# Moving a group of conditioning products from the first layer's mixer into the second layer's attention

## The reference

```python
for l in range(DEPTH):
    mod = (silu_c @ ada_w[l] + ada_b[l])[:, None, :]
    sh1, sc1, g1, sh2, sc2, g2 = jnp.split(mod, 6, axis=-1)
    ...
    h_lat = modulate(x, sh1, sc1)
    h_ctx = modulate(ctx, csh1, csc1)
    ...                                   # l = 0: GLA and convolution, l = 1: attention
    x = x + g1 * o_lat
    ...
    y = hier_moe(modulate(x, sh2, sc2).reshape(-1, d_), *moe_params)
```

## Time and profile before

| | us |
|---|---|
| median of 3 runs | 1013.79 |
| lowest, highest run | 1010.34, 1020.07 |
| span of the profiled execution, first to last instruction | 1008.5 |
| TensorE busy in it | 945.0 (94%) |
| VectorE busy | 621.0 (62%) |
| ScalarE busy | 182.2 (18%) |
| mean granted TensorE clock | 0.980 |

### The profile page before, as it was taken

The page is one execution under the profiler, slowest core; times in us unless marked ns, Lnnn a source line. Parts: engine busy times, 40 slices in busy tenths (PEclk is TensorE's granted clock), DMA queues, the critical chain, the costliest instruction groups (busy, mean ns, idle before and its releaser), DMA issues.

```text
span 1008.5 us, 19757 instructions
## 1 busy us (share of the span) xinstructions
PE 945.0 (94%) x7936; PEld 565.7 (56%) x7936; DVE 621.0 (62%) x1522; ACT 182.2 (18%) x343; POOL 115.0 (11%) x176
## 2 busy tenths in 40 slices
PE   3999999999998999999998999998998899998986
PEld 1443433456445788988888974445645455554532
DVE  1100699869546696676766636567337877776563
ACT  2200022156024010000000014236423000000001
POOL 7100100100500100000001223100101000000000
PEclk9999999999999699999999999999999899999998
DMA  9999957356736899999999968846035899999994
GB/s 332 397 387 369 385 204 297 121 216 251 223 130 228 305 367 338 399 412 408 400 398 401 424 246 327 299 166 251 4 130 209 337 410 405 392 385 409 421 427 163
DMA packets 51645, 311.99 MB, mean 309 GB/s; under 512 B 7128, under 2 KB 8920, under 8 KB 34176
## 3 DMA queue, kind: packets, MB, share of 16 engines
q1 hardware_dynamic: 37040, 277.88, 70.3%
q0 software_dynamic: 9376, 21.19, 6.8%
q10 hardware_dynamic: 5168, 12.06, 3.2%
HBM read 300.52 MB, written 17.25 MB: 315 GB/s over the span
## 4 chain that ended last, share of the span: by engine, by line
PE 74%; DMA 13%; DVE 8%; SPq 2%; issue 1%; ACT 1%; ACTq 0%; POOLq 0%; POOL 0%; DVEq 0%
PE ps L628 49%; DMA ring<-in_moe_w_gate 10%; PE ps L1074 10%; PE ps L641 3%; PE ps L967 3%; PE ps L1117 3%; DMA ring<-in_ada_w 2%; PE ps L1206 2%; SPq L533 2%; PE ps L1461 1%; PE ps L903 1%; DVE xh L1919 1%; PE ps L1430 1%; DMA ar<-h_rows,sm 1%; PE ps L1241 0%
## 5 line engine op out<-in xcount | busy, mean ns | idle before, releaser
L628 PE MATMUL ps<-ring,ar 128*32 128x384 f32 (+6 forms) x3872 | 478.9, 466 | 13.3 <-DMA ring<-in_moe_w_gate 9.7
L628 PEld LDWEIGHTS ps<-ring,ar 128*32 128x32 f32 (+2 forms) x3872 | 197.2, 121 | 142.0 <-issue 82.9
L1074 PE MATMUL ps<-ring,ar 128*32 128x128 f32 x1488 | 167.6, 275 | 0.0
L1074 PEld LDWEIGHTS ps<-ring,ar 128*32 128x32 f32 x1488 | 163.7, 111 | 2.5
L2228 DVE STREAM_TRANSPOSE ar<-ar 32x256 f32<-32x256 f32 x304 | 132.2, 435 | 5.6 <-issue 0.6
L628 PE MATMUL ps<-xh,ring 128*128 128x512 f32 x256 | 114.9, 604 | 0.7 <-DMA ring<-in_even_w_in 0.7
L2271 DVE TENSOR_TENSOR ar<-ar,ps 128x384 f32<-128x384 f32 (+2 forms) x33 | 15.9, 482 | 129.9 <-PE ps L1074 68.3
L628 PE MATMUL ps<-ring,xh 128*128 128x512 f32 x192 | 84.6, 595 | 1.0 <-ACT xh L1521 0.7
L628 PEld LDWEIGHTS ps<-xh,ring 128*128 128x128 f32 x256 | 48.3, 193 | 64.1 <-issue 63.2
L2400 DVE SCALAR_TENSOR_TENSOR ar<-ar,cpar 128x512 f32<-128x512 f32 x120 | 79.6, 742 | 0.0
L1576 ACT ACTIVATE ar<-ps 128x384 f32<-128x384 f32 (+2 forms) x33 | 14.3, 432 | 286.9 <-PE ps L628 202.6
(11 more groups left out here) (394 smaller groups left out, 934.9 us busy)
## 6 DMA issues: line engine op xcount, KB each, us to landing
ring<-in_moe_w_gate SPq DMA_DIRECT2D x31, 2048.0 KB, 18.5
ring<-in_moe_w_up SPq DMA_DIRECT2D x30, 2048.0 KB, 19.6
ring<-in_moe_w_down SPq DMA_DIRECT2D x30, 2048.0 KB, 20.5
ring<-in_ada_w SPq DMA_DIRECT2D x24, 2048.0 KB, 10.4
ring<-in_even_w_in SPq DMA_DIRECT2D x5, 2048.0 KB, 13.9
y_rows<-ar POOLq DMA_DIRECT2D x17, 384.0 KB, 10.5
ring<-in_odd_w_in SPq DMA_DIRECT2D x3, 2048.0 KB, 18.1
y_rows<-ar ACTq DMA_DIRECT2D x16, 288.0 KB, 8.7
```

The costliest lines, as they stand in the source:

```text
L628: return nc.tensor.matmul(o, l, r, start=start, stop=stop)
L1074: m = nc.tensor.matmul(ps[96:128, bank, g * P:(g + 1) * P], xgT[:, p, c, 32 * g:32 * g + 32], w[:, c, 3 * P:HID], start=c == 0 and g == 0, ...
```

## The change

Group 3's four blocks leave the early part of the stream and are loaded behind the three oin blocks, ahead of oout 0. They are multiplied in units 0 to 3 of the attention, each behind that unit's scores and ahead of its `pv`. VectorE's `ada_added(3)` moves from the first layer's mixer (behind `conv_scaled`) to the end of its unit 4 in the attention. GpSimd's `ada_bias(3)` and `mod_rows(3)` move behind the combination of the first layer's experts, with the gate row's load behind them, and the load of expert 6's up weights also waits until the rows have been stored. Three small tables (the scales of the scores) move out of `silu_c`, which must now live on until the attention, into `sm`. Group 3 accumulates in PSUM bank 6 where it had bank 2, and TensorE waits at unit 5 for `ada_added` ahead of the `pv` that writes there. The other edits renumber the counts that follow from the new order.

```diff
@@ weight_stream
-    freed = ... + ada(1, 0, 1, 2) + ein("qk") + ada(1, 3, 4, 5) + ein("v")
-    freed += ada(1, 6, 7) + ein("r")
+    freed = ... + ada(1, 0, 1, 2) + ein("qk") + ada(1, 3) + ein("v")
+    freed += ein("r")
...
-    loaded += ada(1, 4, 5, 6, 7) + ein("r")
+    loaded += ein("r")
...
-    tail += [("oin", 0, 2), ("oin", 0, 0), ("oin", 0, 1), ("oout", 0, 0), ("oout", 0, 1)] + moe_blocks(1)
+    tail += [("oin", 0, 2), ("oin", 0, 0), ("oin", 0, 1)] + ada(1, 4, 5, 6, 7) + [("oout", 0, 0), ("oout", 0, 1)] + moe_blocks(1)
@@ tiles, banks and counts
-        score_scale, score_minus, head_sums = silu_c[:, 0, 0:16], silu_c[:, 1, 0:16], silu_c[:, 2, 0:8]
+        score_scale, score_minus, head_sums = sm[:, 0:16], sm[:, 16:32], sm[:, 32:40]
...
-        ADA_BANK = (6, 2, 3, 2, 6)
+        ADA_BANK = (6, 2, 3, 6, 6)
...
-        MODS = {1: (0, 1), 2: (1, 0), 4: (1, 1)}
+        MODS = {1: (0, 1), 2: (1, 0), 3: (1, 1)}
+        ADDED = {1: 3, 2: 4, 4: 6, 3: 7}
@@ SP, moe_stream
                     sp.wait_ge(sem("q_rot"), 3)
+                    sp.wait_ge(sem("mod_rows"), MOD_STORED[3])
                     expert_load("u", APART)
@@ TensorE, even_in
                 for n in range(4):
                     project("v", n)
-                    if n < 2:
-                        ada_block(3, n)
                 project("r", 0)
                 project("r", 1)
                 project("t", 0)
-                ada_block(3, 2)
                 project("s", 0)
                 cumulate()
                 project("r", 2)
                 project("t", 1)
-                ada_block(3, 3)
                 project("s", 1)
@@ TensorE, odd_mixer, unit u
                     elif u + 3 < 2 * HEADS:
                         score(u + 3)
+                    if u < 4:
+                        ada_block(3, u)
+                    if u == 5:
+                        pe.wait_ge(sem("ada_added"), ADDED[3])
                     if j == 1 and h >= 1:
                         pv(h - 1, 0)
@@ VectorE
                 conv_scaled()
-                ada_added(3)
                 masked(0)
...
                     if 1 <= u <= 6:
                         second_half(u - 1)
+                    if u == 4:
+                        ada_added(3)
@@ GpSimd
             ada_bias(2)
-            ada_bias(3)
             ada_bias(4)
-            for g in range(1, 4):
+            for g in (1, 2):
                 mod_rows(g)
...
             pool.wait_ge(sem("combined"), NT)
-            pool.dma_start(gb[:, 0, :], gate_row(1, 2, 0).to_broadcast([P, D])).then_inc(sem("gate_in"), 16)
+            ada_bias(3)
...
+            mod_rows(3)
+            pool.dma_start(gb[:, 0, :], gate_row(1, 2, 0).to_broadcast([P, D])).then_inc(sem("gate_in"), 16)
```

More of the change, by code:

```diff
@@ L127, in weight_stream @@
     first = ada(0, 0, 2) + ein("cg") + ada(0, 1, 3)
-    freed = ada(0, 0, 2, 1, 3) + ein("cg") + ada(0, *range(4, 12)) + ein("ca") + ada(1, 0, 1, 2) + ein("qk") + ada(1, 3, 4, 5) + ein("v")
-    freed += ada(1, 6, 7) + ein("r")
+    freed = ada(0, 0, 2, 1, 3) + ein("cg") + ada(0, *range(4, 12)) + ein("ca") + ada(1, 0, 1, 2) + ein("qk") + ada(1, 3) + ein("v")
+    freed += ein("r")
     loaded = first + ein("ca") + ada(0, 4, 5, 6) + ada(0, *range(7, 12)) + ein("qk") + ada(1, 0, 1, 2, 3) + ein("v")
-    loaded += ada(1, 4, 5, 6, 7) + ein("r")
+    loaded += ein("r")
     assert sorted(freed) == sorted(loaded)
     tail = ada(1, 8, 9) + [("eout", 0, 0), ("eout", 0, 1)] + ada(1, 10, 11) + moe_blocks(0)
-    tail += [("oin", 0, 2), ("oin", 0, 0), ("oin", 0, 1), ("oout", 0, 0), ("oout", 0, 1)] + moe_blocks(1)
+    tail += [("oin", 0, 2), ("oin", 0, 0), ("oin", 0, 1)] + ada(1, 4, 5, 6, 7) + [("oout", 0, 0), ("oout", 0, 1)] + moe_blocks(1)
     return freed + tail, loaded + tail, len(freed)
@@ L467, in modrow_of @@
             return modrow[:, 0] if g == 0 else mla[:, (0, 1024, 1536, 0, 512)[g]:][:, 0:512]
-        ADA_BANK = (6, 2, 3, 2, 6)
+        ADA_BANK = (6, 2, 3, 6, 6)
         LATE_BANK = 5
-        MODS = {1: (0, 1), 2: (1, 0), 4: (1, 1)}
+        MODS = {1: (0, 1), 2: (1, 0), 3: (1, 1)}
+        ADDED = {1: 3, 2: 4, 4: 6, 3: 7}
         MOD_STORED, MOD_LOADED, n_rows = {}, {}, 0
-        for g, (_, _, n) in enumerate(ADA_GROUPS[1:], 1):
-            n_rows += 16 * n
+        for g in ADDED:
+            n_rows += 16 * ADA_GROUPS[g][2]
             MOD_STORED[g] = n_rows
@@ L634, in ada_block @@
                 arrived(pe, i)
-                if g == 3 and n == 0:
-                    pe.wait_ge(sem("ada_added"), 3)
                 if g:
@@ L910, in gla @@
                 turn_keys(0)
-                pe.wait_ge(sem("ada_added"), 5)
+                pe.wait_ge(sem("ada_added"), 4)
                 eng, c = taken_count(len(UNITS) - 1)
@@ L929, in gla @@
                 turn_keys(1)
-                pe.wait_ge(sem("ada_added"), 6)
+                pe.wait_ge(sem("ada_added"), 5)
                 scores(1)
@@ L1190, in down @@
                 if l == 0 and isinstance(e, int) and e == 0:
-                    pe.wait_ge(sem("ada_added"), 7)
+                    pe.wait_ge(sem("ada_added"), 6)
                 if not (isinstance(e, int) and e == 0) and not narrow(l, e):
@@ L1876, in ada_added @@
             def ada_added(g, halves=(0,)):
-                dve.wait_ge(sem(f"ada_bias{min(g, 3)}"), 64 if g >= 3 else 16 * ADA_GROUPS[g][2] if g else 32)
+                dve.wait_ge(sem(f"ada_bias{min(g, 3)}"), 64 if g == 3 else 32 if g == 4 else 16 * ADA_GROUPS[g][2] if g else 32)
                 for h in halves:
@@ L2673, in mod_rows @@
                 l, a, n = ADA_GROUPS[g]
-                pool.wait_ge(sem("ada_added"), 7 if g == 4 else g + 2)
+                pool.wait_ge(sem("ada_added"), ADDED[g])
                 for s in range(n // 2):
```

## The result

The changed kernel takes 1023.37 us (median of 19 runs, 1019.07 to 1027.86), the kernel before beside it on the same chip 1017.58 us (19 runs, 1009.54 to 1020.94). The ratio is 1.0069, with a 95% interval of 1.0051 to 1.0087: 7 us slower (5.2 to 8.9), clear of zero, and still within the 1% that the forecast called no change. The forecast was a ratio of 1016.9 / 1013.8 = 1.0031, and its range ended at 1022. Of the 6.5 us between 1016.9 and 1023.4, 3.8 are the level of the kernel before, whose median of 19 runs lies 3.8 above the median of three that the forecast was put on. The other 2.7 are the change by the medians, 5.8 where 3.1 was forecast; by the ratio, which has the interval, it is 7.0.

A forecast was written before the change was run, and what follows sets the result against it. TensorE was taken as the bound in both moved places, loads from 892 on. First mixer -3.6, attention +6.7 and transfers 0 gave +3.1 us, 1013.8 to 1016.9 us; range 1009 to 1022.

The forecast's parts named there:

- the main term: Attention: the four added blocks and the wait for VectorE's addition cost +6.7 us; the same as the second term.
- first term: First mixer: removing four blocks saves 3.6 us, bounds -7.4 and -2, since t0 and s0 then wait for others.
- second term: Attention: four blocks on TensorE and a new wait make it 6.7 us longer.
- The walk: Attention, step by step: units 0 to 3 take 3.13 us each, unit 4's transposes start 6.65 later, nothing catches up.
- The new wait: Attention: VectorE's addition in unit 4 waits for the last block, holding unit 4's transposes until 700.0, 6.65 us later.
- The cheaper rival: Attention: all 2.8 us of idle time filled and the addition hidden, cost 4.6, time 1014.8; attention hides more, chance 0.24.
- the clock falls in the first mixer: First mixer: new waits halve the granted clock, r2 takes twice as long, +7.0, in all +10.1 us; chance 0.06.
- a granted clock under 1 near 200: First mixer: one of the signs named in advance that would show the forecast wrong.
- the early gain: First mixer: the 3.6 us saved there, taken to make the attention's rows earlier by that amount.
- The transfers: Attention and behind: moved loads finish by 721, ahead of the next block at 745, so they cost 0.
- The rival of late transfers: Behind the attention: four expert blocks come in too late, end moves 20.4 us, in all +23.5; chance 0.04.
- Within 1%: Whole kernel: time stays within 1% (10 us) of the kernel before, forecast as no change; chance 0.86.

The follow-up runs named there:

- x3: Changed kernel with VectorE's addition of group 3 at the end of its attention unit 5 instead of unit 4; 1014.93 us, ratio 1.0047.
- x8: The changed kernel, unchanged, for a second profile; 1017.44 us.
- x2: Changed kernel with SP waiting for the last gather of expert rows before it issues the four moved blocks; 1018.26 us, ratio 1.0072.
- x9: Repeat of x3 with more rounds; 1016.67 us, ratio 1.0032.
- x10: x3 with one fill product of 512 columns ahead of the second kv unit alone; 1014.4 us, ratio 1.0018.
- x4: Changed kernel with group 3's four blocks neither loaded nor multiplied, so other experts are chosen in the second layer; 1239.23 us, ratio 1.2265.
- x5: x3 with products nobody reads in the new gaps of the first mixer and ahead of the second kv unit; 1012.8 us, ratio 1.0023.
- x7: x3 with two fill products at each of the four first-mixer places the blocks left; 1017.55 us, ratio 1.0076.
- x1: The kernel before, unchanged, for a second profile; 1010.6 us.
- x6: Kernel before with two fill products in each of attention units 0 to 3 in the place of a block, no addition or loads; 1018.1 us, ratio 1.0078.
- x11: The kernel before, unchanged, for a third profile; 1012.39 us.

## Why the prediction was right or wrong

The sign and the main term were right, the total was too small: +3.1 forecast, +7 measured. The step that failed is the first term, 3.6 us saved in the first mixer: it took s0 and the cumulated decays at their old length, while the clock fell behind the new waits and 0.7 to 2.2 us are saved.

**The attention (second term, +6.7): right.** Measured 7.4 in three profiles. The walk gave 3 units of 3.13 us from the transposes of unit 0 to those of unit 3 (9.4), and 5.5 on to those of unit 4; the trace has 9.85 and 5.78. From there to the scores of unit 8 it is 5.83 us before and after, as the walk said. A block's step was taken as 1.84 and is 1.96 in this place (3.25 less 1.29). The new wait was the one named: VectorE's addition for the last block, and behind it unit 5's row maximum and unit 4's scaling. x3 takes it away by moving the addition alone, and 1.56 us go with it. The cheaper rival, that the attention hides the blocks, expected 4.6; even without the addition's wait it is 5.85, and with bare products 4.65. The 2.8 us of idle time hid 1.5 of the blocks' 7.4, or 2.0 of 7.8 if a block is taken at its step here: the waits ahead of units 2, 3 and 4 (0.33, 0.71 and 0.53 in the kernel before) are gone in x3, the 0.85 ahead of the scores of unit 8 is still there.

**The first mixer (first term, -3.6): the term that failed.** t0 was forecast at 192.6 and starts at 192.7 in x8 and x3 (193.2 in the first profile, where the convolution itself ended 0.5 later). s0 was forecast at 194.4 and starts at 194.5. Up to there all of it holds. Then the decays should have started at 195.65 and taken what they took. They start at 196.05 to 197.3 and take 4.4 to 5.8 us where they took 3.73, since s0 and their first part run at 1.2 GHz. In the seven profiles of changed kernels whose mixer is not filled (after, x8, x2, x3, x9, x10, and x4 with 218.73) the keys are 0.7 to 2.2 us ahead of 219.44, 1.4 in the mean, in place of 3.6. The convolution's end scatters from 192.5 to 193.2 in both kernels. Counted from it, the keys start 26.8 to 26.9 us later in three profiles of the kernel before, 24.7 to 24.8 in after, x8, x2 and x3, and 26.0 to 26.1 in x4, x9 and x10, where the clock is low for longer: 2.1 or 0.8 us are saved, 1.5 in the mean. x5 keeps the clock at 1.00 and has 23.4, which is 3.4 saved.

The rival *the clock falls in the first mixer* had the mechanism, with a chance of 0.06, and a wrong size: it let the lower clock last for all of r2 (+7). In every profile the clock was back ahead of r2, which took 7.03 us as always; what fell under it were s0 and the decays, and in x9 and x10 also t0: 1.4 to 2.9 us in all. The forecast had also named a granted clock under 1 near 200 as a sign of being wrong, and that sign is there. I had held the attention's 2.8 idle us in 18 at clock 1.00 against it. There the idle time lies in pieces of 0.3 to 0.8 us; here 2.0 us stand ahead of t0's 1.07 us of narrow products, and 0.8 more behind them. The Trainium skill (TensorE: Matmul & The Clock Gate, Part 1: The HAM clock gate) has idleness bring the lower clock back; the traces agree, with 0.50 behind these two waits, and 1.00 once x5 or x7 fills them. Idle time is not the whole of it in this case, as the combination of the last experts in x1 shows.

**What came between (nothing in the forecast): partly open.** The forecast held that the early gain carries on unchanged to the attention. To the combination of the last experts it does, within 1 us: 384.1 to 385.0 us from the keys in the changed kernels, 383.1 to 384.6 in the kernel before, the two single events aside. From there to the third kv unit the five profiles of changed kernels without fills take 36.9 to 38.4 us. The kernel before, whose code up to there is also that of x6, takes 33.8 and 34.0 in two profiles and 38.0 and 38.1 in two. Two different things make these numbers. In the changed kernels TensorE waits 1.3 to 2.1 us for the last gathers and then runs 1.7 us longer at the lower clock; in x1 and x11 the clock is low for 10 us from the combination on, which hides the gathers.

The wait itself goes with the change. Among the profiles whose combination ran at full clock, before and x6 wait 0.15 and 0.20 us ahead of the second kv unit, and the five changed ones without fills 1.3 to 2.1. The last gather lands 9.3 and 9.5 us behind its issue in before and x6, and 9.9 to 11.3 in the changed kernels. x2 and x4 show that the moved loads are not what delays it, and x10 that 1.7 us of the loss are the clock; what does delay it stays open. How often the other case comes, the low clock in the combination (2 of 4 profiles with the code of before, 1 of 9 with changed code), single profiles can't settle either. By the stages the sum is -1.5 + 7.4 = +5.9 without this part, and 7.0 [5.2, 8.9] was measured, so its share is between -0.7 and +3.0. The means of the profiles that there are, 36.0 for before against 37.5, and 0.7 lost on the way to the combination, would make it +2.2 (an estimate from few profiles).

**The transfers (0): right.** DMA was at 1.02 in the 20 us up to 720 and at 0.60 in the 20 behind, down 0 was issued 34 us behind 720, and the last stage takes 306 to 310 us with and without the change. The rival of late transfers is out.

**The chances.** Within 1% had 0.86, and that is where it is (1.0069); the runs resolve more than the 1% that the forecast took, since the interval is 0.2% to either side. The range held the forecast's own cases but gave the clock too little, and took the level of before from three runs: in the four groups of runs the median of the kernel before was 1009.4 to 1017.6.

No kernel of the study beats the kernel before. The best were x10 and x5, whose intervals reach 1. The stages say why: a block costs 5.85 / 4 = 1.46 us in the attention, and gives back 3.6 / 4 = 0.9 in the mixer at best. That moving only one or two of the four would do better is not excluded by these means, and wasn't tried.

## What to carry to other kernels

Work that stands in a gap of TensorE does two things: it fills the gap, and it keeps TensorE's clock up. Whoever removes it pays for the wait that it covered and for the products that follow at half speed; so price a removed filler with the clock of the next few us, not of the next unit. When work is put between pieces of a chain in which two engines take turns, first look where the other engine has to pick it up: the addition one unit later was worth 1.6 us. And where a stretch has idle time in pieces, only a part of it hides anything: here 1.5 to 2.0 of 2.8 us.

## What the runs showed of the hardware

The granted clock was at 1.00 or 0.50 in nearly every window of 1 us of these stretches, with one value between them where it changes: in x8 down within 194 to 195, up within 197 to 198. When it drops varies between executions of nearly the same code in front of it (x8 within 194 to 195, x9 at about 193), and so does how long it stays low (3 to 4 us in x8, 6 to 7 in x9), and with both the length of t0, s0 and the decays.

The lower clock also came in a stretch in which TensorE was hardly idle. In x1, x11 and x5 it fell about 5 us behind the start of the combination of the last experts, with TensorE idle for 0.06 us in the 4 us ahead of it, and came back some 10 us later; in the other ten profiles the same products ran at full clock and took 8.04 to 8.07 us. In the kernel before this costs 4.2 us each time, and spreads the stage's time from 33.8 to 38.1 us. What brings it is not shown.

A gather of 128 rows that GpSimd issued while SP had three blocks of weights under way landed 9.3 to 11.3 us later (615.09 to 624.40 in before, 615.25 to 625.57 in x2, 614.81 to 626.13 in x9). More blocks queued behind those three made no difference that shows: x2 and x4 had none and have 10.3 and 11.3, the kernels with them 9.9 to 11.3.
